# Attention in a two-layer trunk: the last gated chunk as three split products, the block buffer cleared by GpSimd, three taps moved ahead

## What is computed

```
h = rms_norm(x); z = h @ w_in
u = val * sigmoid(gate)                                # 512 channels each
y = depthwise causal conv(u), width 31, + bias; layer norm over groups of 64; silu
attention: q (8 heads x 64), three branches with own k, v (2 heads each):
  compressed: blocks of 32 positions, stride 16, through a small MLP (silu)
  selected blocks, sliding window; merged by per-head sigmoid gates
x = x + concat(conv, attention) @ w_out
h = rms_norm(x)
layer 0: x = x + (silu(h@w1) * (h@w3)) @ w2            # width 2816
layer 1: x = x + sum over top-2 of 8 experts of the same, width 3584
```

## Time and profile before

| | us |
|---|---|
| median of 3 runs | 1467.14 |
| profiled execution | 1472.86 |
| its span | 1471.1 |
| TensorE busy | 1447.4 (98%) |
| VectorE busy | 1188.1 (81%) |
| ScalarE busy | 932.8 (63%) |
| GpSimd busy | 60.4 (4%) |

### The profile page before, as it was taken

The page is one execution under the profiler, slowest core; times in us unless marked ns, Lnnn a source line. Parts: engine busy times, 40 slices in busy tenths (PEclk is TensorE's granted clock), DMA queues, the critical chain, the costliest instruction groups (busy, mean ns, idle before and its releaser), DMA issues.

```text
span 1471.1 us, 18960 instructions
## 1 busy us (share of the span) xinstructions
PE 1447.4 (98%) x7380; PEld 1189.1 (81%) x7380; DVE 1188.1 (81%) x1109; ACT 932.8 (63%) x878; POOL 60.4 (4%) x70
## 2 busy tenths in 40 slices
PE   7999999999999999999999999999999999999998
PEld 6864999998765888888888888888888888888886
DVE  5995545447995788988898898888889888889887
ACT  4273343434373777777777777777777777777774
POOL 1042000000141000000000000000000000000000
PEclk9999999999999899999999999999999999999999
DMA  7750755532822799999999999999999999999993
GB/s 245 231 170 34 253 188 185 172 115 89 278 94 82 274 363 375 369 363 354 339 364 369 376 351 365 370 336 364 369 369 363 356 371 330 365 376 364 367 368 132
DMA packets 203853, 426.62 MB, mean 290 GB/s; under 512 B 7410, under 2 KB 48626, under 8 KB 203764
## 3 DMA queue, kind: packets, MB, share of 16 engines
q1 hardware_dynamic: 202448, 424.90, 80.6%
q10 hardware_dynamic: 1316, 0.49, 0.1%
HBM read 424.31 MB, written 1.05 MB: 289 GB/s over the span
## 4 chain that ended last, share of the span: by engine, by line
PE 87%; DVE 11%; issue 1%; ACT 1%; DMA 1%; ACTq 0%; POOL 0%; DVEq 0%
PE bank L1922 14%; PE bank L1924 14%; PE bank L1923 14%; PE bank L1944 7%; PE bank L1946 7%; PE bank L1945 7%; DVE arena L990 6%; PE bank L1826 3%; PE bank L1828 3%; PE bank L1827 3%; PE bank L1655 2%; PE bank L1456 2%; PE bank L1932 2%; PE bank L1843 1%; PE bank L1844 1%; PE bank L1845 1%
## 5 line engine op out<-in xcount | busy, mean ns | idle before, releaser
L961 DVE TENSOR_TENSOR w_split<-ring,w_split 128x2048 fp32r<-128x2048 f32 x369 | 843.7, 2290 | 192.6 <-ACT w_split L585 191.0
L585 ACT CAST w_split<-ring 128x2048 fp32r<-128x2048 f32 x369 | 706.0, 1914 | 295.6 <-PE bank L1924 161.6
L1922 PE MATMUL bank<-w_split,xe_hi 128*128 128x512 f32 x896 | 355.0, 396 | 0.0
L1924 PE MATMUL bank<-w_split,xe_lo 128*128 128x512 f32 x896 | 349.7, 390 | 0.0
L1923 PE MATMUL bank<-w_split,xe_hi 128*128 128x512 f32 x896 | 348.9, 389 | 0.0
L1924 PEld LDWEIGHTS bank<-w_split,xe_lo 128*128 128x128 f32 x896 | 168.2, 188 | 36.3
L1922 PEld LDWEIGHTS bank<-w_split,xe_hi 128*128 128x128 f32 x896 | 168.3, 188 | 34.9 <-DVE w_split L961 1.2
L1923 PEld LDWEIGHTS bank<-w_split,xe_hi 128*128 128x128 f32 x896 | 168.5, 188 | 33.2
L1944 PE MATMUL bank<-w_split,actT_hi 128*128 128x512 f32 x448 | 175.2, 391 | 0.0
L1946 PE MATMUL bank<-w_split,actT_lo 128*128 128x512 f32 x448 | 174.5, 389 | 0.0
L1945 PE MATMUL bank<-w_split,actT_hi 128*128 128x512 f32 x448 | 174.4, 389 | 0.0
(11 more groups left out here) (239 smaller groups left out, 1424.1 us busy)
## 6 DMA issues: line engine op xcount, KB each, us to landing
ring<-in_moe_w SPq DMA_DIRECT2D x336, 1024.0 KB, 5.8
ring<-in_dense_w SPq DMA_DIRECT2D x33, 1024.0 KB, 5.4
ring<-in_w_in SPq DMA_DIRECT2D x8, 1024.0 KB, 9.5
ring<-in_w_in SPq DMA_DIRECT2D x4, 2048.0 KB, 8.2
ring<-in_w_out SPq DMA_DIRECT2D x4, 2048.0 KB, 7.9
ring<-in_cmp_k_w SPq DMA_DIRECT2D x2, 2048.0 KB, 14.0
ring<-in_cmp_v_w SPq DMA_DIRECT2D x2, 2048.0 KB, 9.3
ring<-in_w_in SPq DMA_DIRECT2D x2, 1120.0 KB, 12.5
```

The costliest lines, as they stand in the source:

```text
L585: nc.scalar.copy(split_part(0, t), raw(t)).then_inc(w_hi_ready, 1)
L961: V.tensor_tensor(split_part(1, t), raw(t), split_part(0, t).bitcast(F32), ALU.subtract).then_inc(w_lo_ready, 1)
L1922: T.matmul(dst, xe_hi[:, kk, own], hi[:, k, :], start=(kk == 0), stop=False)
L1924: last = T.matmul(dst, xe_lo[:, kk, own], hi[:, k, :], start=False, stop=(kk == KD - 1))
```

## The change

- Chunk 3 of the gated part is split as chunks 1 and 2 are. Its high and low parts lie in the memory of `hT_hi` and `hT_lo`. ScalarE makes the high part after the sigmoid of chunk 0, VectorE the low part after the gate of chunk 0. `glu_product` needs no new code, as it takes the split path for each chunk that is in `glu_hi`; the semaphore counts go from 4 to 6 a layer.
- The clear of the block buffer goes from VectorE to GpSimd, as the first instruction of a layer there, ahead of `norm`. In layer 1 it waits for the last dense product.
- The taps are issued by a function for one tap of one chunk, and three taps of chunk 0 are issued before the gate of chunk 1. `conv_taps` leaves out taps that are already made.

```diff
+        glu_hi[3], glu_lo[3] = [a[:].rearrange("p k t -> p (k t)").rearrange("p (h k n) -> p h k n", h=2, k=KD)
+                                for a in (hT_hi, hT_lo)]
@@ GpSimd
+                if l > 0:
+                    pl.wait_ge(w_used, BASE)
+                nc.gpsimd.memset(blkT[:], 0.0).then_inc(blk_clear, 1)
                 norm(2 * l)
@@ ScalarE
                 gate_of_glu(0)
+                glu_high(3)
                 gate_of_glu(1)
@@ VectorE
+                def next_tap(c):
+                    tap = tap_of[c]
+                    w = p_(l, "conv_w", c * TAPS + tap)
+                    if tap == 0:
+                        dv.wait_ge(u_ready, CC * l + c + 1)
+                        V.tensor_scalar(y[:, c, :], u[:, c, 0:S], w, p_(l, "conv_b", c), ALU.mult,
+                                        ALU.add).then_inc(conv_step, 1)
+                    else:
+                        dv.wait_ge(conv_step, last_step[c])
+                        V.scalar_tensor_tensor(out=y[:, c, :], in0=u[:, c, tap:tap + S], scalar=w,
+                                               in1=y[:, c, :], op0=ALU.mult, op1=ALU.add).then_inc(conv_step, 1)
+                    conv_n[0] += 1
+                    tap_of[c], last_step[c] = tap + 1, conv_n[0]
+
                 def conv_taps(c0, taps):
-                    if taps[0] == 0:
-                        dv.wait_ge(u_ready, CC * l + c0 + 2)
                     for tap in taps:
                         for c in (c0, c0 + 1):
...
+                            if tap_of[c] <= tap:
+                                next_tap(c)
...
                 glu_low(1)
                 glu_low(2)
-                V.memset(blkT[:], 0.0).then_inc(blk_clear, 1)
                 glu(0)
+                glu_low(3)
+                for _ in range(3):
+                    next_tap(0)
                 glu(1)
                 conv_taps(0, range(0, 2))
@@ TensorE, glu_product
-                            pe.wait_ge(glu_lo_ready, 4 * l + 2 * (c - 1) + half + 1)
+                            pe.wait_ge(glu_lo_ready, 6 * l + 2 * (c - 1) + half + 1)
```

More of the change, by code:

```diff
@@ L976, in glu @@
                     V.tensor_tensor(u[:, c, PAD:], bank[GLU_BANK[c]][:, 0:S], sig[:, c % 2, :], ALU.mult).then_inc(u_ready, 1)
+                tap_of, last_step = [0] * CC, [0] * CC
+                def next_tap(c):
[11 more added lines that the diff above has]
+                    tap_of[c], last_step[c] = tap + 1, conv_n[0]
                 def conv_taps(c0, taps):
-                    if taps[0] == 0:
-                        dv.wait_ge(u_ready, CC * l + c0 + 2)
                     for tap in taps:
                         for c in (c0, c0 + 1):
[L984 to L993, removed]
+                            if tap_of[c] <= tap:
+                                next_tap(c)
                 def attention_low(i, h):
@@ L1007, in glu_low @@
                     for half in range(2):
-                        dv.wait_ge(glu_hi_ready, 4 * l + 2 * (c - 1) + half + 1)
+                        dv.wait_ge(glu_hi_ready, 6 * l + 2 * (c - 1) + half + 1)
                         V.tensor_tensor(glu_lo[c][:, half], view("win", l, half)[:, :, c * P:(c + 1) * P],
```

## The result

| | before | changed |
|---|---|---|
| median, 20 runs each | 1467.24 us | 1473.14 us |
| lowest to highest | 1465.32 to 1473.16 | 1469.37 to 1476.82 |
| profiled execution, its span | 1472.86, 1471.1 | 1475.84, 1474.1 |

The ratio is 1.0035, 95% interval 1.0025 to 1.0045: 3.7 to 6.6 us slower. The forecast was 1467.4 in a range to 1471.8, so it was wrong. The attention stages moved almost as forecast; the time was lost at a place that the prediction had ruled out, just before the last scatter.

What follows compares the result with a forecast made beforehand. VectorE was taken as the bound from chunk 3's gate to the convolution's end. Terms -0.48 (layer 0), -0.48 (layer 1) and +1.25 (clear) gave +0.3 us on the 1467.14 median, so 1467.4 us; range 1463.0 to 1471.8.

Steps and rivals of the forecast that it cites:

- The three terms that were forecast: Chunk 3's gate earlier in layers 0 and 1, -0.48 us each; GpSimd clear delaying layer 1's row scaling, +1.25; sum +0.3.
- Chunk 3 saves 1.10 us of TensorE a layer: Gated part, each layer: chunk 3 as three float32r products takes 5.80 us of TensorE, not 6.90.
- by 0.48 us, and no further, as VectorE itself is then the late one: Chunk 3's gate: moves from 41.66 to 41.18, limited by VectorE's four taps before it; ends 0.39 and 1.10 us.
- the 40.9 that the text gave as a sign against itself: Layer 0, chunk 3's gate: forecast at 41.2; the forecast is wrong if it comes before 40.9.
- The split's work lies in idle time, 0.9 to spare: VectorE before chunk 1's gate: two subtractions (2.36 us) and three taps (1.5) fit in 3.57 us of idle.
- The taps pay nothing, VectorE waits ahead of z's low part: Behind chunk 1's gate: VectorE arrives 1.2 us early, waits for ScalarE's copy; value 0, ends 0 and 1.25 per layer.
- The rival in which they pay: Attention stages: VectorE's total work counts and moved taps pay too; -2.2 us, 1464.9 us; chance 0.13.
- The clear costs 1.25 in layer 1, 1.1 to 1.4: Start of layer 1: GpSimd's clear ahead of the norm's power delays VectorE's row scaling by 1.25 us, uncovered.
- The rival without cost: Start of layer 1: GpSimd's clear is done before VectorE's additions; only -0.96 us remains, 1466.2 us; chance 0.12.
- the port rival: Start of layer 1: VectorE's additions wait for the clear, row scaling 0.7 us later than forecast; 1468.1 us; chance 0.05.
- The clock falls in layer 1, chance 0.20, +3.5: Start of layer 1: added TensorE idle lowers the granted clock, slowing chunk 0's product; +3.5 us, 1470.9 us; chance 0.20.
- The signs that the text named: Trace signs in layers 0 and 1: chunk 3's duration, VectorE idles, gate times, clear's delay, clock between 338 and 350.

Runs made afterwards that it cites:

- e1: Changed kernel plus 192 never-executed TensorE instructions in the skipped conditional body ahead of the last scatter; median 1468.95 us, ratio 0.9995 to the kernel before.
- e7: Kernel before with only three taps of chunk 0 moved ahead of chunk 1's gate; 1465.47 us in one run.
- e8: Kernel before with only the block buffer's clear moved to GpSimd, ahead of the norm; 1467.81 us in one run.
- e10: Changed kernel plus 128 never-executed TensorE instructions in the skipped body ahead of the last scatter; 1467.78 us in one run, kernel before 1469.71.
- e3: Changed kernel with GpSimd's clear placed behind both powers of the norm instead of ahead; 1472.01 us, ratio 1.0022 to the kernel before.
- e4: Changed kernel with the clear behind the norm's powers and 192 never-executed TensorE instructions ahead of the last scatter; 1469.78 us, ratio 0.9998 to the kernel before.

## Why the prediction was wrong

The step that failed is its first: "The expert and dense stages are matmuls end to end and the change touches none of them, so the question is only what the two attention stages do". No instruction there was edited, but all of TensorE's code behind chunk 3 was moved, by 32 instructions from layer 0 on and by 64 from layer 1 on. That cost 3.05 us of fetch and 0.97 of granted clock, 4.0 together. Take it off the +4.3 and +0.3 is left, which is the forecast. The three terms that were forecast give -0.47 - 0.47 + 1.17 = +0.23; that the rest, -0.17 and -0.15 in the attention stages and +0.36 in the experts, comes to nothing is luck. e1, with nothing but the code's place changed, gives -0.7 us (-2.3 to +1.0) against before. None of the rivals had this mechanism, and the range ended 1.3 us below the median.

Step by step:

- *Chunk 3 saves 1.10 us of TensorE a layer*: it saved 1.45. It was sized by chunks 1 and 2, which take 5.8 each; in the changed trace their products start 0.118 us apart, those of chunk 3 0.114, and why is not shown. The surplus has no effect: "by 0.48 us, and no further, as VectorE itself is then the late one". Measured 0.47 in each layer, and no idle before the gate. Layer 0's gate came at 40.78 and so before the 40.9 that the text gave as a sign against itself, but the whole stage had begun 0.40 earlier in this execution; the distance is what counts.
- *The split's work lies in idle time, 0.9 to spare*: 0.70 left. In layer 0 the two subtractions began at 24.16, the taps ended at 27.9 (28.1 forecast).
- *The taps pay nothing, VectorE waits ahead of z's low part*: the new idle is there, 0.4 ahead of each of two low parts (about 1 ahead of one was forecast), and e7 puts the value at 0.00. The rival in which they pay is out.
- *The clear costs 1.25 in layer 1, 1.1 to 1.4*: 1.17 to 1.18, four times (changed, e1, e8, e10). The memset took 1.80 (1.79 forecast). The rival without cost is out. So is the port rival at the place where it was told, VectorE's additions; VectorE was held up by the clear in e3 and e4 instead, at the row scaling.
- *The clock falls in layer 1, chance 0.20, +3.5*: with the clear ahead of the norm, in one of four traces (e1, not the changed kernel, e8, e10), for 1.1 us, and there it slowed the transposes and not chunk 0's product. The product was slowed in e3 alone, by 1.7. In the six traces without added idle time at that place it never fell. The rival can happen, and its price was put two to three times too high. In the changed kernel it was in the last scatter that the clock fell, and an unforeseen wait set it off.
- The signs that the text named all lie in the edited stages. The granted clock stayed at 1.00 between 338 and 350, as asked, and the forecast was wrong all the same.

What would have shown it ahead of time: the page of before has the instruction queue, and its trace has a jump of 3.5 us that ends 0.5 us before the scatter starts. A fetch was hidden there, with 0.4 us to spare.

**Open.** The expert stage is 0.3 us longer in each kernel with chunk 3's split, and 0.28 of it is at a single place, where TensorE waits for a low part of the weights: the product at 916.99 starts 0.57 us behind the one before it, in the kernel before 0.29. Ahead of it ScalarE's copy at 909.02 has 0.28 of idle with "issue" as its releaser, which the kernel before has not. That ScalarE's code was being fetched is argued, and was not tried. The 0.15 gained behind chunk 3's gate in each layer has no cause shown. And the stretch from the projection to the last dense product takes 200.85 us in before, changed and e4, but 196.3 to 197.2 in all the others, and each part of the change is found on the low side. The granted clock is 1.00 in both. It varies between executions by up to 4.6 us, and what sets it is open. Likewise the routing takes 22.2 to 25.0 us by how often the granted clock falls in it, in kernels that don't differ there.

## What to carry to other kernels

A change that adds instructions moves all the code behind it. Where an engine jumps, count by how much, and look at how much of the wait after the jump is cover: here 64 instructions in the attention stages cost 4 us at the very end. The trace has the jump itself and the first instructions behind it. If a difference has "issue" as its releaser and one place, pad a body that is never executed before looking for a reason in the edit itself. And a clear given to an idle engine is free only by its place: ahead of a short instruction that others wait for it cost 1.17 of its 1.80 us, and beside VectorE's row scaling the same.

## What the hardware showed beyond that

- A jump of TensorE over code took 3.4 to 3.9 us, of which a start 2 us ahead of the last product and a wait for VectorE hid all. The wait from product to product around it had two levels, 2.05 to 2.2 us and 4.6 to 5.3, the first for displacements of 0, 32, 192 and 256 instructions, the second for 64. Two packets of code came 3.1 to 3.9 us apart, and the first product behind a needed packet started 1.4 us behind its end.
- In the changed kernel the granted clock fell to 0.50 behind 4.7 us without a product, and stayed there for the products of the scatter: 0.97 us on top. In the kernel before, with 1.67 us of idle there, it stayed at 1.00.
- A VectorE row scaling (one SBUF input) under a GpSimd memset of 2048 columns took 1.92 in place of 0.75. Subtractions with two SBUF inputs (0.62 each), and additions with one PSUM operand, were not slowed by the same memset.
- Three float32r products in place of one float32 product are the faster way at 256 columns: 48 of them, some 0.114 us each, took 5.45 us in chunk 3 (5.8 in chunks 1 and 2), the float32 ones 6.90.
